# Opening of a one-core transformer block: the order of the first loads, and the first two weight units' products run pair by pair

## The reference

```
mod_l = silu(c) @ mod_w + mod_b          # 6 x 1024 wide, for the tokens
mod_c = silu(c_ctx) @ mod_w + mod_b      # the same for the context
h_lat = rms_norm(x, norm_g[0])   * (1 + mod_l[scale]) + mod_l[shift]
h_ctx = rms_norm(ctx, norm_g[0]) * (1 + mod_c[scale]) + mod_c[shift]
z = h @ gla_w_in                         # keys, queries, values, gate, low rank
```

## Time and profile before

| | |
|---|---|
| runs | 1620.04, 1621.49, 1621.49 us (median 1621.49) |
| profiled execution | 1619.98 us, of which the span in the trace is 1618.2 us |
| TensorE busy | 1597.1 us (99% of the span) |
| weight load of TensorE | 1356.2 us (84%) |
| VectorE busy | 837.9 us (52%) |
| ScalarE busy | 494.0 us (31%) |
| GpSimd busy | 128.9 us (8%) |
| granted clock of TensorE over the span | 0.999 |

### The profile page before, as it was taken

The page is one execution under the profiler, slowest core; times in us unless marked ns, Lnnn a source line. Parts: engine busy times, 40 slices in busy tenths (PEclk is TensorE's granted clock), DMA queues, the critical chain, the costliest instruction groups (busy, mean ns, idle before and its releaser), DMA issues.

```text
span 1618.2 us, 19903 instructions
## 1 busy us (share of the span) xinstructions
PE 1597.1 (99%) x8110; PEld 1356.2 (84%) x8110; DVE 837.9 (52%) x1017; ACT 494.0 (31%) x564; POOL 128.9 (8%) x112
## 2 busy tenths in 40 slices
PE   8999999999999999989999999999999999999998
PEld 6899999888888888878888888888988888888887
DVE  5897754674334344465444534346457445444444
ACT  4553264522212233332222222221223212212222
POOL 0100000020000000020000003135006000000000
PEclk9999999999999999999999999999999999999999
DMA  9544511212222223313222223332212322222332
GB/s 385 185 163 158 207 53 53 78 63 94 104 104 85 84 88 91 121 55 110 95 104 100 75 91 91 111 144 104 79 53 78 104 104 80 101 104 65 98 99 77
DMA packets 30345, 171.38 MB, mean 106 GB/s; under 512 B 3152, under 2 KB 5456, under 8 KB 16592
## 3 DMA queue, kind: packets, MB, share of 16 engines
q1 hardware_dynamic: 25936, 153.80, 27.5%
q0 software_dynamic: 4352, 16.78, 3.1%
HBM read 168.47 MB, written 2.10 MB: 105 GB/s over the span
## 4 chain that ended last, share of the span: by engine, by line
PE 94%; DVE 2%; DMA 2%; issue 1%; ACT 1%; SPq 0%; POOL 0%; POOLq 0%; DVEq 0%
PE bank L499 93%; DMA mod_w<-in_mod 2%; ACT w_hi L1170 0%; DVE mod_sum L1602 0%; DVE a_lo L2015 0%; SPq L339 0%; PE bank L799 0%; DVE w_lo L1963 0%; DVE tmp L2024 0%; PE bank L743 0%; POOL xT L438 0%; DVE a_lo L2044 0%; DVE w_lo L1581 0%; DVE xT L1997 0%; DVE y_gla L1994 0%
## 5 line engine op out<-in xcount | busy, mean ns | idle before, releaser
L1581 DVE TENSOR_TENSOR w_lo<-w_raw,w_hi 128x2048 fp32r<-128x2048 f32 x142 | 327.9, 2309 | 386.9 <-ACT w_hi L1170 386.8
L499 PE MATMUL bank<-a_hi,w_hi 128*128 128x512 f32 x1248 | 488.5, 391 | 5.1 <-DVE a_lo L2044 2.4
L499 PE MATMUL bank<-a_hi,w_lo 128*128 128x512 f32 x1248 | 485.7, 389 | 0.0
L499 PE MATMUL bank<-a_lo,w_hi 128*128 128x512 f32 x1248 | 485.6, 389 | 0.0
L1170 ACT ACTIVATE w_hi<-w_raw 128x2048 fp32r<-128x2048 f32 x144 | 275.5, 1913 | 557.8 <-PE bank L499 557.6
L499 PEld LDWEIGHTS bank<-a_hi,w_hi 128*128 128x128 f32 x1248 | 234.3, 188 | 57.3 <-issue 5.9
L499 PEld LDWEIGHTS bank<-a_hi,w_lo 128*128 128x128 f32 x1248 | 234.2, 188 | 48.5
L499 PEld LDWEIGHTS bank<-a_lo,w_hi 128*128 128x128 f32 x1248 | 234.3, 188 | 48.3 <-issue 0.5
L499 PE MATMUL bank<-g_hi,w_hi 128*128 128x512 f32 (+1 forms) x538 | 207.2, 385 | 0.0
L499 PE MATMUL bank<-g_hi,w_lo 128*128 128x512 f32 (+1 forms) x538 | 207.2, 385 | 0.0
L499 PE MATMUL bank<-g_lo,w_hi 128*128 128x512 f32 (+1 forms) x538 | 207.2, 385 | 0.0
(11 more groups left out here) (290 smaller groups left out, 1603.5 us busy)
## 6 DMA issues: line engine op xcount, KB each, us to landing
w_raw<-in_ffn_in SPq DMA_DIRECT2D x66, 1024.0 KB, 4.8
w_raw<-in_ffn_out SPq DMA_DIRECT2D x24, 768.0 KB, 4.2
mod_raw<-in_mod POOLq DMA_DIRECT2D x16, 1024.0 KB, 5.5
w_raw<-in_ffn_out SPq DMA_DIRECT2D x24, 640.0 KB, 3.9
w_raw<-in_gla_in SPq DMA_DIRECT2D x12, 1024.0 KB, 4.9
w_raw<-in_mix_in SPq DMA_DIRECT2D x10, 1024.0 KB, 4.8
mod_w<-in_mod SPq DMA_DIRECT2D x8, 1024.0 KB, 18.1
w_raw<-in_gla_out SPq DMA_DIRECT2D x4, 1024.0 KB, 4.8
```

The source lines that it names most:

```text
L499: return pe.matmul(out, lhs, rhs, start=first, stop=last, skip_group_check=True)
L1581: V.tensor_tensor(flat(w_lo[s]), flat(w_raw[s]), flat(w_hi[s]).bitcast(F32), ALU.subtract).then_inc(lo_done[s], 1)
```

## The change

Loads: after x come the modulation weights of pair 0, then both weight units, then pairs 1, 2 and 3. ScalarE copies the first rows ahead of the first upper split, and makes the second unit's upper split right after the first pair's activations. VectorE's lower split of the first unit is cut in two halves (`first_lower`), one between the scaling and the lower activations of pair 0 and one behind them, followed by the lower split of the second unit; a new semaphore `first_lo` tells of the first half. TensorE broadcasts the roots after the modulation products of pair 0, then does, for each pair, the parts of both units. The parts of pair 1 to 3 follow in an order written out by hand. The rows of odd pairs go through bank 5 and no longer bank 4, which the second unit now fills. The counts of the dummy products change.

```diff
@@ SyncE @@
-            sp.dma_start(flat(w_raw[0]), a["gla_in"][0]).then_inc(raw_loaded[0], 16)
-            for p in range(3):
+            load_mods(0)
+            for s in range(2):
+                sp.dma_start(flat(w_raw[s]), a["gla_in"][s]).then_inc(raw_loaded[s], 16)
+            for p in range(1, 4):
                 load_mods(p)
-            sp.dma_start(flat(w_raw[1]), a["gla_in"][1]).then_inc(raw_loaded[1], 16)
-            load_mods(3)
@@ TensorE @@
-                b = (2, 4)[p % 2]
+                b = (2, 5)[p % 2]
...
-            keep_busy(7, 32)
+            keep_busy(7, 29)
             pe.wait_ge(streamed_sum, KD)
             token_sums(6, 0, sq_sum, T, True, True).then_inc(sums_ready, 1)
             keep_busy(7, 5)
-            first_roots(6, PAIRS, 1)
             pe.wait_ge(wide_set, 2)
             mod_lines(0)
+            first_roots(6, PAIRS, 1)
             pe.wait_ge(turn_set, 3)
             mod_columns(0)
-            keep_busy(5, 4)
+            keep_busy(5, 12)
+            pe.wait_ge(first_lo, 1)
+            k_part(0, (0, 1))
             mod_lines(1)
             pe.wait_ge(lo_done[0], cnt.next(lo_done[0]))
-            for p in range(1, 4):
-                k_part(0, (2 * p - 2,))
-                mod_columns(p)
-                k_part(0, (2 * p - 1,))
-                if p < 3:
-                    mod_lines(p + 1)
             pe.wait_ge(lo_done[1], cnt.next(lo_done[1]))
-            k_part(1, range(4))
-            k_part(0, (6, 7))
+            k_part(1, (0,))
+            mod_columns(1)
+            k_part(1, (1,))
+            keep_busy(2, 6)
+            k_part(0, (2,))
+            mod_lines(2)
+            k_part(0, (3,))
+            k_part(1, (2,))
+            mod_columns(2)
+            k_part(1, (3,))
+            mod_lines(3)
+            k_part(0, (4,))
+            mod_columns(3)
+            k_part(0, (5,))
+            k_part(1, (4, 5))
+            k_part(0, (6,))
             pe.wait_ge(streamed_sum, 2 * KD)
             token_sums(5, 0, dec_k[1], TC, True, True).then_inc(sums_ready, 1)
-            k_part(1, (4, 5))
+            k_part(0, (7,))
+            k_part(1, (6,))
             first_roots(5, TC // P, 2)
-            k_part(1, (6, 7))
+            k_part(1, (7,))
@@ ScalarE @@
             stream_squares(xT, T, range(KD))
+            copy_rows(0)
             split_hi(0)
-            copy_rows(0)
             first_his(0)
+            split_hi(1)
             copy_rows(1)
             first_his(1)
             copy_rows(2)
-            split_hi(1)
             first_his(2)
@@ VectorE @@
             V.tensor_copy(x_var[:], col4[:, 0:PAIRS])
-            split_lo(0)
...
+            def first_lower(part):
+
+                if part == 0:
+                    dve.wait_ge(hi_done[0], cnt.next(hi_done[0]))
+                w = slice(part * UNIT // 2, (part + 1) * UNIT // 2)
+                V.tensor_tensor(flat(w_lo[0])[:, w], flat(w_raw[0])[:, w], flat(w_hi[0])[:, w].bitcast(F32),
+                                ALU.subtract).then_inc((first_lo, lo_done[0])[part], 1)
...
+                if p == 0:
+                    first_lower(0)
                 for m in (CPU * p, CPU * p + 1):
                     dve.wait_ge(norm_hi, cnt.next(norm_hi))
...
                 first_norm(p)
-                if p == 2:
+                if p == 0:
+                    first_lower(1)
                     split_lo(1)
```

More of the change, by code:

```diff
@@ L249, in build @@
         raw_loaded = [sem(f"raw_loaded{s}") for s in range(2)]
+        first_lo = sem("first_unit_first_half_lo_done")
         hi_done = [sem(f"weight_hi_done{s}") for s in range(2)]
@@ L1199, in copy_rows @@
                 act.wait_ge(rows_ready, p + 1)
-                nc.scalar.activation(mod_rows[p % 2][:], bank[(2, 4)[p % 2]][:], ACT.Copy).then_inc(rows_copied, 1)
+                nc.scalar.activation(mod_rows[p % 2][:], bank[(2, 5)[p % 2]][:], ACT.Copy).then_inc(rows_copied, 1)
             def first_his(p):
```

## The result

The changed kernel takes 1628.54 us (median of 6, from 1626.90 to 1631.79) against 1621.49 (median of 6). The ratio is 1.005, with a 95% interval of 1.0038 to 1.0061: slower, by 7.05 us between the medians. The forecast was slower, 1626.0, with a range that ends at 1628.5. The direction is right; the time lies just outside the range and 2.2 us beyond the sum of 4.8, and the profile shows a reason at once.

The account below looks back on a forecast made before the run. TensorE's own work and its idle moments before 36 us bound the opening; low-rank product 4.0 us late plus a 0.8 us second wait gave +4.8 on the 1621.49 median, about 1626.0, range 1621.5 to 1628.5.

Parts of the forecast that it names:

- the sum of 4.8: Opening: low-rank product 4.0 us late plus 0.8 at the second wait, 4.8 us slower in total.
- First product 23.1: TensorE's first real product, on the first unit, at 23.1 us against 24.44: 1.3 us won.
- columns: TensorE's turning products of each pair; pair 1 forecast at 29.4 us, pair 2 at 39.5, pair 3 (last) at 45.25.
- sums asked for at 51.6: TensorE reaches the wait for VectorE's context square sums at 51.6 us; done at 54.2, so it idles 2.6.
- second wait: TensorE at its second context-key product waits 0.8 us for a bank held until VectorE's lower parts of the low-rank result.
- low-rank product 59.3: TensorE's low-rank product, behind the context sums and three k-parts, starts at 59.3 us instead of 55.27, 4.0 late.
- second context-key product: TensorE gets there at 73.3 us and waits until 74.1 for its bank; before it stood at 69.34.
- The step called decisive: Four more k-parts (5.4 us) and pair 1's modulation products (1.9) ahead of the last columns, 45.25 instead of 38.48 us.
- Rival D: Clock falls in the 2.6 us context wait; three k-parts at half rate cost another 4 us, some 1630; chance 0.05.
- the three dummy products taken away there: Start, before VectorE's first sums of squares: three fewer dummies cost nothing; if not covered, 0.4 us.
- 1.5 us of dummy products at 31.7 us: Twelve dummy passes before unit 0's chunk 2 k-part, while VectorE's lower part is awaited until 33.15; 1.5 us lost.
- upper bound of 6.5: Upper bound on the slowdown: each of four stages built from steps may slip 0.3 to 0.5 us, about +6.5.

Follow-up runs that it names:

- the filled kernel: Changed kernel with ten dummy products in TensorE's wait for the context's square sums; 1626.58 us, ratio 1.004; run again 1626.60, ratio 1.0037.
- the second and the sixth experiment: Changed kernel with modulation of pairs 2 and 3 ahead of three k-parts: 1623.67; pushed further, replacing six dummy products, VectorE reordered too: 1620.11, ratio 0.9998.
- the two here: Changed kernel with three first dummy products given back, alone: 1628.00 us; with ten dummies in the context wait as well: 1626.94.
- the two experiments made from it: Kernel before with context sums asked for three k-parts earlier: 1625.27, ratio 1.0027; kernel before with the changed load order alone: 1623.16, ratio 1.0014.
- the first dummies back: Changed kernel with 32, not 29, dummy products before the wait near 13 us; 1628.00 us, ratio 1.0043.
- the filled kernels: Changed kernel with ten dummies in the context wait: 1626.58 and 1626.60; with VectorE's lower parts moved: 1624.82, single execution; with three first dummies back: 1626.94.
- both edits: Changed kernel with three first dummy products given back and ten dummy products in the context wait; 1626.94 us, ratio 1.0034.
- the half filled: Changed kernel with five dummy products in the wait for the context's square sums; 1628.08 us, ratio 1.0044.

## Why the prediction was nearly right and still missed

**Right, step by step.** First product 23.1 (23.14); pair 1's products 26.05 and its columns 29.4 (29.43); columns of pair 2 at 39.5 (39.54) and of pair 3 at 45.25 (45.30); sums asked for at 51.6 and had at 54.2 (54.32, with a wait of 2.5 for 2.6); second wait 0.8 (0.7); low-rank product 59.3 and second context-key product 74.1 wherever the clock stays up (59.19 and 74.10). The sum of 4.8 us is measured: 4.9 in the changed kernel's own trace up to the sums behind the second context-key product, and 4.7 and 4.9 as whole times of the filled kernel, between single executions with no slow stretch in the opening (1624.70 and 1624.89 against 1619.98). The step called decisive, the late place of the last columns, is what the second and the sixth experiment turn round.

**Rival D was given 0.05 and happened in half of the profiled executions.** The prediction kept the clock out of the sum: the rows of before show 1.00 throughout with waits up to 1.0 us, it noted that the new wait was 2.6, and it took the absence of a fall in one profiled execution for near certainty. That is the step that failed. What stands in its place: of six profiled executions of the changed kernel three had half the clock behind the context wait, which cost 3.2 us in the first and 1.6 in the two others. Four had it from about 14 to 17 or 21 us, behind the wait for VectorE's first sums, for another 1.6 or 3.2; the prediction put that wait and the three dummy products taken away there at nothing, and no rival has a fall there. The Trainium skill, "TensorE: Matmul & The Clock Gate", section "Part 1: The HAM clock gate (the "warmup" mystery)", says that idling brings the clock down to half. The runs agree in part: half of the changed kernel's profiled executions show it behind the 2.5 us wait and half don't, and the kernel before shows it once it is made to wait (0.67 granted from 48 to 52 us). The price of D was put at 4 us when it happens, three k-parts at half rate; the clock came back before all three were done, and it was 3.2 once and 1.6 to 1.8 in the other cases. The medians stand 7.05, 7.57 and 7.59 over before, where the order alone gives 4.8.

**The numbers drawn from the sum.** 1621.49 and 4.8 are 1626.3, and the prediction wrote about 1626.0; its upper bound of 6.5 gives 1628.0, and the range was drawn to 1628.5. Neither changes the account: the measured 1628.54 is beyond both.

**What the change wanted and did not get.** 1.3 us earlier at the start were won. They were spent on 1.5 us of dummy products at 31.7 us and on the wait for the context sums.

**Open.** In the profiled executions, what the changed kernel has over 4.8 us at the end of the opening is slow clock, by the table above. What makes a fall come in one execution and not in the next isn't shown. Near 13 us it came behind five of the six waits of 1.25 us or more (1.25 to 1.74; 1.56 was the one without) and behind none of the eleven that were shorter or absent. Five of twelve profiled executions with 29 dummy products have it there and none of five with 32 (the two here, the kernel before and the two experiments made from it); with so few, and a median that moves by 0.2, the three dummies aren't shown to be the cause. Filling the context wait takes 1.2 us (1627.79 to 1626.60) and, with the first dummies back, 1.1 (1628.00 to 1626.94) in the medians, with intervals that overlap; the filled kernels' medians stay 5.3 to 6.4 over before, although none of their profiled executions has a slow stretch in the opening, and where the rest lies isn't known.

Behind 80 us, all six profiled executions of the changed kernel have slow clock near 330 us and four near 705, and end 0.6 to 1.9 further behind than they stand at 80; the one of the kernel before has none there. Other executions of the kernel before have mean clocks of 0.995 to 0.998 and a median 1.5 above that one (0.2 to 1.3 in the later comparisons), so they lose time to the clock as well, at places that no trace shows. The execution with both edits that took 1626.89, at a mean clock of 0.995, was 1.9 over the one at 0.999.

## What to carry to other kernels

When two chains share an engine, look for the last step of the shorter chain: moving useful work ahead of it costs nothing on the busy engine at that place, and comes back where the chains meet (here 7.3 us of work ahead of the last columns put them 6.8 us later, and 4.8 us reached the end). A new wait of TensorE in a list of dense products is worth its length plus, in part of the executions, a stretch at half clock behind it (1.6 or 3.2 us here, in four of seven profiled executions with the same 2.5 us wait); put the second term into the sum, not only into a rival. One profiled execution at a clock of 1.00 doesn't tell that the clock is safe: read the mean clock of every execution.

## What the runs showed of the hardware

- The granted clock fell to half behind a wait of TensorE of 2.5 us in 3 of 6 profiled executions of one and the same kernel, in the one with three more dummy products at the start, and in the one of the kernel before with such a wait. Waits of 1.3 to 1.7 us near 13 us were followed by it in five (four of the changed kernel, one of the half filled), and not in the first, which had 1.6 there; the wait of 1.2 us at 23 us never was.
- The slow stretches of the opening were 3.4 or 6.8 us long, and cost 1.6 or 3.2 us.
- Executions of the kernel before with a mean clock of 0.999 took 1619.6 to 1620.8 us, those at 0.995 up to 1622.67: a large part of the spread of this kernel is the clock.
- At half clock the 128x512 products start 0.43 us apart instead of 0.23, and the 16 modulation products of one load take 1.93 instead of 1.07.
- A 2.5 us gap filled with 128x128 products of constants costs nothing, and the clock stayed up in all we have: the sums behind it come at the same time (54.03 filled, 54.04 unfilled), and none of the four profiled executions of the filled kernels had low clock behind it.
